# First norm's sums read apart from the keys', its factors turned by transposes, class-order factors from diagonals, first transfers reordered

## Chip, cores, metric

The kernel runs on one core of a Trainium2 chip. The metric is the device time of one execution in microseconds (us), the median of several.

## What is computed

Two transformer blocks follow one another on one sequence of 512 tokens with 1,024 features, all in float32. The part that the change touches is the first norm, the queries and keys of the first attention, and every later norm of the same form:

```python
h = rmsnorm(x, norm_mix_g[i])          # x * rsqrt(mean(x*x) + eps) * g
z = h @ w_in[i]                        # queries, keys, values, gates of both mixers
qa, ka, va, qb, kb, vb, ga, gb = jnp.split(z, split_at, axis=-1)
y_a = mixer_a(qa, ka, va, q_norm_g[i], k_norm_g[i], ...)   # q and k normed by head, rotary, 2 key heads
y_b = mixer_b(qb, kb, vb, rel_bias)    # dilated attention: token 4 l + r belongs to class r
x = x + (gate_a * y_a + gate_b * y_b) @ w_out[i]
# then a relu^2 MLP, an embedding gate, and the second block: SwiGLU, retention and
# differential attention, attention to a memory, SwiGLU, each behind an rmsnorm
```

## The kernel before

Features lie on the partitions, tokens along the free axis. A float32 product is made of three matmuls on halves of both operands: high by high (L637, or L646 where tokens are the output's partitions), high by low (L640, L649), low by high (L643, L652). ScalarE makes a weight's high half (L719), VectorE the low half (L728), a block of eight k-steps at a time (1 MB by SyncE's queue, two buffers each way). Block 0 holds the two key heads ("ka"), block 1 the values ("va", 32 steps of three 128x256 matmuls), block 2 the first two query heads.

The norm factor r of a token is not applied to x: projections are made of x times the gain, and r comes in when a product is drained. For the first norm ("mix") ScalarE squares the eight tiles of x (L1134), VectorE adds them into ACC (L1149, event x_acc). TensorE then turns ACC into sums, a column of 128 tokens at a time: four matmuls against a column of ones in token order (L932), four in class order, whose stationary operand is every fourth column of ACC (L936), and four for each key head (L942). All sixteen columns lie in PSUM bank 7 under one name, ("sums", "mix"), and VectorE reads them from L959 on, followed by a root by three Newton steps on 16 columns (L1018 to L1038). For the tile RB, which holds the factors of all 512 tokens on every partition, VectorE splits r in two halves and spreads the high half over the identity (`dve_rows`, L983 to L987), ScalarE does so with the low half (`act_rows`, L996), and TensorE multiplies both by a matrix of ones (L948, L951; for the keys L1275, L1278; L2099, L2102 for the two norms that share one place). ScalarE copies the result into RB (L1005). There are ten such pairs of row matmuls in the program: one each for mix, mlp, ple, mx2, mq and f2, one for each key head, and two for "both".

The order on every engine is written by hand. Each stream (a generator) yields a place, a number on the scale of the blocks, before its next instructions, and `weave` issues the instructions of the stream with the smallest place; `US` is a microsecond on that scale. So an instruction waits behind all that its engine has at smaller places. PSUM banks are claimed in the order of issue on TensorE:

```python
def claim(self, name, *banks):
    ...
    earlier = [self.before[b] for b in banks if b in self.before]
    for b in banks:
        self.before[b] = (self.sig.sem(f"free{own}"), self.turns[own])
    return earlier
```

The first writer of a new name waits until the last name in that bank has been drained (semaphore free7 for bank 7). `norm_place("mix")` is 1.88; the key heads' rotation starts at place 1.02 (`key_place`), with VectorE's steps L1211 and L1215 and ScalarE's L1185 (square), L1189 and L1190 (halves swapped), GpSimd's L1203.

SyncE issues the first transfers in `sp_begin`: the first quarter of the key weights, gains, second quarter, x tiles 1, 2 and 3, the other half of the weights, x tiles 4 to 7, block 1's weights, then small constants, the rotary table, the identity and ones, the bias selectors and table. ScalarE's queue brings x tile 0.

Of the kernel before, what the change touches and what calls it, by code (L numbers as in the profile page):

```python
# [10 lines left out]
R32 = mybir.dt.float32r  # L11
# [4 lines left out]
P = 128  # L16
# [237 lines left out]
class Kernel:  # L254
# [70 lines left out]
    def memory(self):  # L325
# [10 lines left out]
        self.RB, self.RBr, self.ACC = sb(86.5, [P, S]), sb(86.5, [P, S], R32), sb(88.5, [P, S])  # L336
        self.tmp = [sb(90.5 + 2 * i, [P, S])[:, :] for i in range(2)]
        self.tmp_r = [sb(90.5 + 2 * i, [P, S], R32)[:, :] for i in range(2)]
# [16 lines left out]
        self.qs_r = [pa(68 + 2 * i, [P, S], R32)[:, :] for i in range(2)]  # L355
        self.key_sq = [pa(76 + 2 * i, [P, S])[:, :] for i in range(2)]
        self.key_lo = [pa(80 + 2 * i, [P, S], R32)[:, :] for i in range(2)]
# [37 lines left out]
        self.ACC2, self.RB1, self.RB1r = pa(106, [P, S]), pa(108, [P, S]), pa(108, [P, S], R32)  # L395
# [39 lines left out]
        norm = lambda n: {"v": tiny(n), "r": tiny(n), "ev": tiny(n), "a": tiny(n), "h": tiny(n), "rh": tiny(4), "rl": tiny(4)}  # L435
        four = lambda: {k: tiny(4) for k in ("v", "r", "a", "h", "n")}
        self.nm = {"mix": norm(16), "mlp": norm(4), "ple": norm(4), "both": norm(8)}
        self.part, self.rh1, self.rl1 = tiny(4), tiny(4), tiny(4)
        self.ka_n = [{"rh": tiny(4), "rl": tiny(4)} for _ in range(2)]
# [483 lines left out]
    def pe_norm(self, pe, new, v, place, heads=()):  # L923

        yield place
        for w in new(self.at("ones"), *self.claim(("sums", v), 7)):
            pe.wait_ge(*w)
        out = self.bank(("sums", v))
        for w in new(self.absorbed(v, KT - 1)):
            pe.wait_ge(*w)  # L930
        for n in range(4):
            done = pe.matmul(out[:, n:n + 1], self.ACC[:, n * P:(n + 1) * P], self.ones[:, 0:1], start=True, stop=True)  # L932
        if heads:
            yield place + 0.12
            for n in range(4):
                pe.matmul(out[:, 4 + n:5 + n], class_of(self.ACC[:, :], n), self.ones[:, 0:1], start=True, stop=True)  # L936
            for j, sq in enumerate(heads):
                yield self.norm_place(v) + 0.06 * (j - 1)
                for w in new(self.at("head_sq", j)):
                    pe.wait_ge(*w)  # L940
                for i in range(4):
                    done = pe.matmul(out[:, 8 + 4 * j + i:9 + 4 * j + i], sq[:, i * P:(i + 1) * P], self.ones[:, 0:1], start=True, stop=True)  # L942
        done.then_inc(*self.full(("sums", v)))
        yield self.norm_place(v) + (6 if v == "mix" else 5) * US
        for w in new(self.at("rows_hi", v), *self.claim(("rows", v), 7)):
            pe.wait_ge(*w)
        out = self.bank(("rows", v))
        pe.matmul(out, self.ones_r, self.RBr[:, :], start=True, stop=False)  # L948
        for w in new(self.at("rows_lo", v)):
            pe.wait_ge(*w)  # L950
        pe.matmul(out, self.ones_r, self.tmp_r[0], start=False, stop=True).then_inc(*self.full(("rows", v)))  # L951

    def dve_norm(self, dve, new, v, place, rb_before):
# [4 lines left out]
        if v == "mix":  # L958
            dve.tensor_scalar(q["v"][:, 0:8], out[:, 0:8], 1.0 / D, EPS, ALU.mult, ALU.add).then_inc(*self.up("vector"))  # L959
            for w in new(self.sig.now("vector")):  # L960
                dve.wait_ge(*w)
            dve.tensor_scalar(q["ev"][:, 0:4], q["v"][:, 0:4], EPS, None, ALU.mult).then_inc(*self.up("ev", v))
            for w in new(self.at("ev", v)):
                dve.wait_ge(*w)
            for j in range(2):
                c = slice(8 + 4 * j, 12 + 4 * j)
                done = dve.scalar_tensor_tensor(out=q["v"][:, c], in0=out[:, c], scalar=1.0 / 128, in1=q["ev"][:, 0:4],
                                                op0=ALU.mult, op1=ALU.add)
            done.then_inc(*self.drained(("sums", v)))
        else:  # L970
            dve.tensor_scalar(q["v"], out[:, 0:4], 1.0 / D, EPS, ALU.mult, ALU.add).then_inc(*self.drained(("sums", v)))
        for w in new(self.cleared(("sums", v))):
            dve.wait_ge(*w)
        yield from self.dve_rsqrt(dve, new, q, place)
        for w in new(self.at("inverse", id(q))):
            dve.wait_ge(*w)
        yield from self.dve_rows(dve, new, q["rh"], q["rl"], q["r"][:, 0:4], self.RBr[:, :], ("rows_hi", v), ("rl_made", v),
                                 rb_before, place)

    def dve_rows(self, dve, new, rh, rl, r, rows, made, low_made, rows_before, place):  # L980

        yield place
        dve.tensor_scalar(rh.bitcast(R32), r, 1.0, None, ALU.mult).then_inc(*self.up("vector"))  # L983
        for w in new(self.sig.now("vector"), *rows_before):
            dve.wait_ge(*w)
        dve.tensor_tensor(rl, r, rh, ALU.subtract).then_inc(*self.up(*low_made))
        dve.tensor_tensor(by_token(rows), self.ident.unsqueeze(1).broadcast_to([P, 4, P]), spread4(rh),  # L987
                          ALU.mult).then_inc(*self.up(*made))

    def act_rows(self, act, new, rl, low_made, rows, made, rows_before, place):  # L990

        yield place
        for w in new(self.at(*low_made), *rows_before):
            act.wait_ge(*w)
        for i in range(4):
            done = act.activation(rows[:, i * P:(i + 1) * P], self.ident, ACT.Copy, scale=rl[:, i:i + 1])  # L996
        done.then_inc(*self.up(*made))

    def act_norm(self, act, new, v, place):
        yield from self.act_rows(act, new, self.nm[v]["rl"], ("rl_made", v), self.tmp_r[0], ("rows_lo", v),  # L1000
                                 [self.absorbed(v, 6)], place)
        yield place + (2.6 if v == "mix" else 2) * US
        for w in new(self.filled(("rows", v))):
            act.wait_ge(*w)
# [67 lines left out]
    def sp_begin(self, sp, new):  # L1072
# [36 lines left out]
    def act_begin(self, act, new):  # L1109
        yield -3.0  # L1110
        act.dma_start(self.X[:, 0:1, :], self.io["xT"].rearrange("(k p) s -> p k s", p=P)[:, 0:1, :]).then_inc(*self.up("x0", by=16))
        for w in new(self.at("zeros")):
            act.wait_ge(*w)
# [78 lines left out]
    def qs_free(self, n):  # L1192
# [3 lines left out]
        return self.filled(("rows_k", n - 2)) if n < 4 else self.at("joined", n - 2)  # L1196
# [2103 lines left out]
```

## Time and profile before

| | us |
|---|---|
| median of 3 runs | 2027.58 (2025.69 to 2027.70) |
| the profiled execution's own time | 2025.08 |
| its span in the profile | 2023.2 |
| TensorE busy | 2006.6, 99% of the span |
| VectorE busy | 1433.7, 71% |
| ScalarE busy | 989.0, 49% |
| GpSimd busy | 306.7, 15% |
| mean granted TensorE clock | 0.998 of full |

The profile is one execution. Busy time of TensorE counts a matmul until its last column has left the array, so consecutive matmuls overlap in it: the pace of the engine is the distance from start to start. Times of a row count from the start of the span.

### The profile page before, as it was taken

The numbers are of one execution on the slowest core, as the hardware profiler recorded it, in microseconds if no ns is written. First come the engines' busy times: TensorE is split into PE (matmuls) and PEld (weight loads), VectorE is DVE, ScalarE is ACT, GpSimd is POOL, SyncE is SP. The second block draws the span as 40 slices with busy tenths as digits, with TensorE's granted clock in tenths as the row PEclk, the third lists the DMA queues.
The fourth block names the chain that finished last, engine by engine and source line by source line (L and its number), as shares of the span: only waits on it lengthen the run. The fifth ranks groups of instructions, "written<-read, shape, count | busy, mean of one in ns | idle before, by whom it ended". The sixth has DMA issues, their size and how long they took to land.

```text
span 2023.2 us, 30620 instructions
## 1 busy us (share of the span) xinstructions
PE 2006.6 (99%) x11818; PEld 1758.6 (87%) x11818; DVE 1433.7 (71%) x2722; ACT 989.0 (49%) x1901; POOL 306.7 (15%) x494
## 2 busy tenths in 40 slices
PE   9999999999999999999999999999999999999998
PEld 8788898888889988888999989978898888999987
DVE  7886557676667776678788766676876668777765
ACT  6656334455445444555444434555554446444433
POOL 0230000021000000231011013422551021101110
PEclk9999999999999999999999999999999999999999
DMA  6141422122333333322323323222342123233341
GB/s 196 45 154 44 128 84 87 63 86 82 104 94 102 112 94 109 105 84 94 104 95 109 100 91 118 80 68 95 103 157 85 43 83 100 94 98 107 104 136 42
DMA packets 194665, 196.23 MB, mean 97 GB/s; under 512 B 5068, under 2 KB 189708, under 8 KB 194444
## 3 DMA queue, kind: packets, MB, share of 16 engines
q1 hardware_dynamic: 193800, 193.22, 29.8%
q8 instruction: 94, 1.54, 0.3%
q10 hardware_dynamic: 720, 1.05, 0.2%
q14 instruction: 51, 0.42, 0.1%
HBM read 192.05 MB, written 6.93 MB: 98 GB/s over the span
## 4 chain that ended last, share of the span: by engine, by line
PE 90%; DVE 5%; POOL 2%; issue 1%; ACT 1%; DMA 0%; SPq 0%; DVEq 0%; POOLq 0%; ACTq 0%
PE ps L700 19%; PE ps L637 18%; PE ps L643 18%; PE ps L640 18%; PE ps L646 3%; PE ps L649 3%; PE ps L652 3%; DVE m L728 1%; PE ps L1359 1%; PE ps L1657 1%; PE ps L1666 1%; PE ps L2260 0%; PE ps L1369 0%; PE ps L1371 0%; PE ps L1370 0%
## 5 line engine op out<-in xcount | busy, mean ns | idle before, releaser
L637 PE MATMUL ps<-m,m 128*128 128x512 f32 x1728 | 684.8, 396 | 0.0
L643 PE MATMUL ps<-m,m 128*128 128x512 f32 x1728 | 674.6, 390 | 0.2 <-DVE m L1161 0.2
L640 PE MATMUL ps<-m,m 128*128 128x512 f32 x1728 | 674.0, 390 | 0.0
L719 ACT ACTIVATE m<-m 128x512 fp32r<-128x512 f32 x512 | 306.8, 623 | 272.9 <-PE ps L643 234.4
L728 DVE TENSOR_TENSOR m<-m,m 128x512 fp32r<-128x512 f32 x512 | 382.2, 758 | 48.7 <-ACT m L719 47.0
L700 PEld LDWEIGHTS ps<-m,m 128*128 128x128 f32 x3276 | 398.3, 192 | 3.4 <-issue 0.4
L700 PE MATMUL ps<-m,m 128*128 128x256 f32 x3276 | 399.4, 283 | 0.2 <-ACT m L866 0.2
L643 PEld LDWEIGHTS ps<-m,m 128*128 128x128 f32 x1728 | 324.6, 188 | 70.8 <-DVE m L1161 1.1
L637 PEld LDWEIGHTS ps<-m,m 128*128 128x128 f32 x1728 | 325.4, 188 | 64.8 <-issue 1.5
L640 PEld LDWEIGHTS ps<-m,m 128*128 128x128 f32 x1728 | 325.5, 188 | 62.2 <-DVE m L728 0.3
L774 DVE TENSOR_TENSOR m<-m,m 128x512 fp32r<-128x512 f32 x273 | 198.8, 748 | 87.0 <-ACT m L764 86.5
L764 ACT ACTIVATE m<-m 128x512 fp32r<-128x512 f32 x273 | 159.6, 620 | 79.3 <-DVE m L787 25.8
L646 PE MATMUL ps<-m,m 128*128 128x256 f32 (+1 forms) x548 | 161.9, 295 | 0.0
L649 PE MATMUL ps<-m,m 128*128 128x256 f32 (+1 forms) x548 | 158.1, 289 | 0.5 <-DVE m L728 0.5
L652 PE MATMUL ps<-m,m 128*128 128x256 f32 (+1 forms) x548 | 157.9, 288 | 0.0
L1993 POOL TENSOR_TENSOR m<-m,m 128x512 f32<-128x512 f32 x44 | 75.3, 1713 | 531.8 <-DVE m L1960 284.8
L918 POOL TENSOR_TENSOR m<-m,m 128x512 f32<-128x512 f32 x35 | 47.9, 1369 | 459.6 <-ACT m L902 459.3
L646 PEld LDWEIGHTS ps<-m,m 128*128 128x128 f32 x548 | 104.7, 191 | 2.4 <-issue 0.4
L649 PEld LDWEIGHTS ps<-m,m 128*128 128x128 f32 x548 | 104.7, 191 | 2.5 <-DVE m L728 0.9
L652 PEld LDWEIGHTS ps<-m,m 128*128 128x128 f32 x548 | 104.5, 191 | 1.1
L866 ACT ACTIVATE m<-ps 128x256 f32<-128x256 f32 x117 | 44.8, 383 | 120.0 <-PE ps L700 120.0
L1785 DVE TENSOR_TENSOR m<-m,ps 128x512 f32<-128x512 f32 x72 | 49.2, 683 | 58.8 <-PE ps L643 58.7
(375 smaller groups left out, 2270.8 us busy)
## 6 DMA issues: line engine op xcount, KB each, us to landing
m<-ffn_w SPq DMA_DIRECT2D x44, 1024.0 KB, 5.1
m<-w_in SPq DMA_DIRECT2D x28, 1024.0 KB, 5.0
m<-ffn_w SPq DMA_DIRECT2D x24, 768.0 KB, 4.5
m<-w_ff SPq DMA_DIRECT2D x16, 1024.0 KB, 5.5
m<-w_ff SPq DMA_DIRECT2D x16, 768.0 KB, 4.4
m<-w_in SPq DMA_DIRECT2D x17, 512.0 KB, 5.0
m<-w_out SPq DMA_DIRECT2D x8, 1024.0 KB, 5.1
m<-mem_w_kv SPq DMA_DIRECT2D x8, 1024.0 KB, 5.4
```

The lines of the kernel that those rows point to most:

```text
L637: pe.matmul(o, lh, xh, start=k == 0, stop=False)
L640: pe.matmul(o, ll, xh, start=False, stop=False)
L643: done = pe.matmul(o, lh, xl, start=False, stop=k == nk - 1)
L646: pe.matmul(o, xh, wh[:, k, c:c + job.width], start=k == 0, stop=False)
L649: pe.matmul(o, xh, wl[:, k, c:c + job.width], start=False, stop=False)
L652: done = pe.matmul(o, xl, wh[:, k, c:c + job.width], start=False, stop=k == nk - 1)
L700: done = pe.matmul(out[half], weight[step == 1][c][:, k, :], xl if step == 2 else xh, start=a == 0 and c in (0, 1, 3), stop=a == 11 and c ...
L719: act.activation(self.WH[b % 2][:, at], self.RAW[b % 2][:, at], ACT.Copy).then_inc(*self.up("w_hi", b, c))
L728: dve.tensor_tensor(self.WL[b % 2][:, at], self.RAW[b % 2][:, at], self.WH[b % 2][:, at].bitcast(F32), ALU.subtract).then_inc(*self.up("w_ ...
L764: act.activation(self.split_slot(b, c, 0), src[c], ACT.Copy).then_inc(*self.up("w_hi", b, c))
L774: dve.tensor_tensor(self.split_slot(b, c, 1), src[c], self.split_slot(b, c, 0).bitcast(F32), ALU.subtract).then_inc(*self.up("w_lo", b, c))
L1993: pool.tensor_tensor(slot, slot, self.RB[:, :], ALU.mult).then_inc(*self.up("h_sum", name, t))
```

## The change

Five edits, in one diff:

- TensorE: the first norm's sums in token order are issued at place 1.42 instead of 1.65, under their own claim of bank 7; the four class-order sums are gone. The key heads' sums keep their places (1.82 and 1.88) but claim bank 7 under a new name, ("key_sums",).
- VectorE: the first norm's read-out and root are on 4 columns and stand at place 1.5, instead of after 1.95; the keys' (8 columns) stand after 1.95.
- The factors are spread by four transposes of one column broadcast to 128x128 (`turn_factors`), with no split in halves; `dve_rows` and `act_rows` are gone for all ten.
- The class-order factors are taken from RB's diagonals by four reductions on VectorE at place 3.6 (L1246).
- Transfers: x tile 1 goes by ScalarE's queue; SyncE waits for the first quarter of the weights before it issues the second half, and for x tiles 4 and 5 before it issues the small constants and what follows.

The diff, cut to what the text speaks of (other places change the names of tiles and columns alone):

```diff
-    def pe_norm(self, pe, new, v, place, heads=()):
+    def pe_norm(self, pe, new, v, place):
...
         for n in range(4):
             done = pe.matmul(out[:, n:n + 1], self.ACC[:, n * P:(n + 1) * P], self.ones[:, 0:1], start=True, stop=True)
-        if heads:
-            yield place + 0.12
-            for n in range(4):
-                pe.matmul(out[:, 4 + n:5 + n], class_of(self.ACC[:, :], n), self.ones[:, 0:1], start=True, stop=True)
-            for j, sq in enumerate(heads):
-                yield self.norm_place(v) + 0.06 * (j - 1)
...
         done.then_inc(*self.full(("sums", v)))
-        yield self.norm_place(v) + (6 if v == "mix" else 5) * US
-        for w in new(self.at("rows_hi", v), *self.claim(("rows", v), 7)):
+        yield self.norm_place(v) + (3 if v == "mix" else 5) * US
+        for w in new(self.at("inverse", id(self.nm[v])), self.at("consts"), *self.claim(("rows", v), 7)):
             pe.wait_ge(*w)
-        out = self.bank(("rows", v))
-        pe.matmul(out, self.ones_r, self.RBr[:, :], start=True, stop=False)
-        for w in new(self.at("rows_lo", v)):
-            pe.wait_ge(*w)
-        pe.matmul(out, self.ones_r, self.tmp_r[0], start=False, stop=True).then_inc(*self.full(("rows", v)))
+        self.turn_factors(pe, self.nm[v]["r"][:, 0:4], ("rows", v))
+
+    def turn_factors(self, pe, r, name):
+        for i in range(4):
+            done = pe.transpose(self.bank(name)[:, i * P:(i + 1) * P], r[:, i:i + 1].broadcast_to([P, P]), self.ident)
+        done.then_inc(*self.full(name))
...
+        dve.tensor_scalar(q["v"], out[:, 0:4], 1.0 / D, EPS, ALU.mult, ALU.add).then_inc(*self.drained(("sums", v)))
...
+    def act_norm(self, act, new, v, place, rb_before):
+        yield place + (-1 if v == "mix" else 2) * US
+        for w in new(self.filled(("rows", v)), *rb_before):
             act.wait_ge(*w)
         act.activation(self.RB[:, :], self.bank(("rows", v)), ACT.Copy).then_inc(*self.drained(("rows", v)))
...
-        sp.dma_start(self.X[:, 1:2, :], x[:, 1:2, :]).then_inc(*up("x1", by=16))
         sp.dma_start(self.X[:, 2:4, :], x[:, 2:4, :]).then_inc(*up("x2", by=16))
+        for w in new(self.at("first_w0")):
+            sp.wait_ge(*w)
         sp.dma_start(raw[:, 4:8, :], w0[:, 4:8, :]).then_inc(*up("first_w2", by=16))
...
         yield -0.9
+        for w in new(self.at("x4")):
+            sp.wait_ge(*w)
         sp.dma_start(self.G[:, n:], io["smalls"][:, n:]).then_inc(*up("smalls", by=16))
...
+        act.dma_start(self.X[:, 1:2, :], ...).then_inc(*self.up("x1", by=16))     # in act_begin, behind x tile 0
...
+    def pe_key_sums(self, pe, new):
+        for j, sq in enumerate(self.key_sq):
+            yield self.norm_place("mix") + 0.06 * (j - 1)
+            if j == 0:
+                for w in new(*self.claim(("key_sums",), 7)):
+                    pe.wait_ge(*w)
...
+    def dve_key_norm(self, dve, new, place):
+        yield place
+        q, out = self.key_n, self.bank(("key_sums",))
+        for w in new(self.filled(("key_sums",)), self.at("ev", "mix")):
+            dve.wait_ge(*w)
...
+        yield from self.dve_rsqrt(dve, new, q, place)
+
+    def dve_class_factors(self, dve, new, place):
+        yield place
+        for w in new(self.rb_made("mix"), self.filled(("sums", "mix"))):
+            dve.wait_ge(*w)
+        for c in range(4):
+            done = dve.tensor_tensor_reduce(self.ACC[:, c * P:(c + 1) * P], class_of(self.RB[:, :], c), self.ident, 1.0, 0.0, ALU.mult,
+                                            ALU.add, self.class_r[:, c:c + 1])
...
-        s += [self.pe_norm(pe, new, v, 1.65 if v == "mix" else self.norm_place(v), heads=self.key_sq if v == "mix" else ()) for v in self.NORMS]
+        s += [self.pe_norm(pe, new, v, 1.42 if v == "mix" else self.norm_place(v)) for v in self.NORMS]
+        s += [self.pe_key_sums(pe, new)]
...
-        s += [self.dve_norm(dve, new, v, self.norm_place(v) + 0.8 * US, self.rb_before(v)) for v in self.NORMS]
+        s += [self.dve_norm(dve, new, v, 1.5 if v == "mix" else self.norm_place(v) + 0.8 * US) for v in self.NORMS]
+        s += [self.dve_key_norm(dve, new, self.norm_place("mix") + 0.8 * US), self.dve_class_factors(dve, new, 3.6)]
```

How the order moves on TensorE between the class-order sums and the first key head's sums. Line numbers of the changed kernel are three lower here; m_91 and m_86 are the first key head's squares, full, free and the like the semaphores waited for. Before:

```order
L652 MATMUL ps<-m_54,m_50 128x256
L936 MATMUL ps<-m_58,m_63 128x1 x4
L646 MATMUL ps<-m_54,m_49 128x256
L649 MATMUL ps<-m_56,m_49 128x256
L652 MATMUL ps<-m_54,m_50 128x256
L646 MATMUL ps<-m_54,m_49 128x256
L649 MATMUL ps<-m_56,m_49 128x256
L652 MATMUL ps<-m_54,m_50 128x256
L942 MATMUL ps<-m_58,m_91 128x1 [waits head_sq]
L942 MATMUL ps<-m_58,m_91 128x1 x3
```

Changed (39 matmuls of the value projection lie between the token-order sums and these rows):

```order
L649 MATMUL ps<-m_54,m_50 128x256
L643 MATMUL ps<-m_54,m_49 128x256
L646 MATMUL ps<-m_56,m_49 128x256
L649 MATMUL ps<-m_54,m_50 128x256
L1221 MATMUL ps<-m_58,m_86 128x1 [waits head_sq,free7]
L1221 MATMUL ps<-m_58,m_86 128x1 x3
```

The class-order sums are gone, and the key sums wait for one semaphore more, free7, in the same place among the projection's matmuls.

VectorE around the read-out of the first norm's sums (L959 before, L947 now). m_60 is the tile of small columns, m_55 the low half of block 2's weights. Before:

```order
L1211 TENSOR_TENSOR m_86<-ps,m_84 128x512 [waits swap,full1]
L1215 TENSOR_TENSOR m_85<-m_85,m_87 128x512 [waits free0,turned]
L1174 TENSOR_SCALAR m_83<-m_83,m_59 128x512 x2
L728 TENSOR_TENSOR m_55<-m_51,m_53 128x512 [waits w_hi]
L1215 TENSOR_TENSOR m_86<-m_86,m_88 128x512 [waits free1,turned]
L728 TENSOR_TENSOR m_55<-m_51,m_53 128x512 [waits w_hi] x2
L959 TENSOR_SCALAR m_60<-ps 128x8 [waits full7]
```

Changed:

```order
L1167 TENSOR_TENSOR m_83<-ps,m_81 128x512 [waits swap,full1]
L1171 TENSOR_TENSOR m_82<-m_82,m_84 128x512 [waits free0,turned]
L1130 TENSOR_SCALAR m_80<-m_80,m_59 128x512 x2
L725 TENSOR_TENSOR m_55<-m_51,m_53 128x512 [waits w_hi]
L1171 TENSOR_TENSOR m_83<-m_83,m_85 128x512 [waits free1,turned]
L947 TENSOR_SCALAR m_60<-ps 128x4 [waits full7]
L951 TENSOR_SCALAR m_60<-m_60 128x4 [waits free7]
```

The read-out stands two weight subtractions earlier, directly behind the second key head's rotation; all that is ahead of that is unchanged.

## Rows read from the trace of the kernel before

**Rows 1.** The page: busy time of each engine and its share of the span.

```profile
PE 2006.6 (99%) x11818; PEld 1758.6 (87%) x11818; DVE 1433.7 (71%) x2722; ACT 989.0 (49%) x1901; POOL 306.7 (15%) x494
```

**Rows 2.** Waits of TensorE, first 70 us (total, times, longest).

```profile
PE ps L1223 <- DVE m L1254: 0.4, 1, 0.4
PE ps L1359 <- DVE m L1397: 0.4, 1, 0.4
```

**Rows 3.** Chain that ended last (start us, us, what), first 50 us.

```profile
28.56 1.75 PE ps L936 x8
...
31.13 0.79 PE ps L942 x8
...
36.90 0.68 DVE m L987
...
46.04 0.14 issue
46.18 1.02 PE ps L1223 x8
```

**Rows 4.** Timeline of TensorE, 23 to 46 us (start us, us, engine, line, ...).

```profile
23.55 0.28 PE L646 MATMUL ps<-m,m 128*128 128x256 f32 x1
...
30.96 0.28 PE L942 MATMUL ps<-m,m 128*128 128x1 f32 x2
...
45.35 0.39 PE L643 MATMUL ps<-m,m 128*128 128x512 f32 x1
```

**Rows 5.** Timeline of VectorE, 20 to 34 us.

```profile
21.35 1.48 DVE L1149 TENSOR_TENSOR m<-m,m 128x512 f32<-128x512 f32 x2
26.08 0.69 DVE L1211 TENSOR_TENSOR m<-ps,m 128x512 f32<-128x512 f32 x1 [3.25 <-ACT m L1190]
...
31.07 0.68 DVE L1215 TENSOR_TENSOR m<-m,m 128x512 f32<-128x512 f32 x1
31.67 1.28 DVE L728 TENSOR_TENSOR m<-m,m 128x512 fp32r<-128x512 f32 x2
33.55 0.17 DVE L959 TENSOR_SCALAR m<-ps 128x8 f32<-128x8 f32 x1 [0.60 <-PE ps L942]
```

**Rows 6.** Timeline of ScalarE, 21 to 28 us.

```profile
24.12 0.63 ACT L719 ACTIVATE m<-m 128x512 fp32r<-128x512 f32 x1 [2.74 <-DMA m<-w_in]
```

**Rows 7.** Timeline of SyncE and ScalarE at the start: issues, and work on x tile 4.

```profile
10.71 1.34 ACT L1119 ACTIVATE m<-m,m 128x512 fp32r<-128x512 f32 x2 [0.74 <-DMA m<-xT]
...
13.52 0.37 SPq L879 DMA_DIRECT2D m<-w_in  x1
```

**Rows 8.** Timeline of TensorE: row matmuls, and four transposes in the attention.

```profile
39.32 0.39 PE L948 MATMUL ps<-m,m 128*128 128x512 f32 x1
...
39.77 0.39 PE L637 MATMUL ps<-m,m 128*128 128x512 f32 x1
...
61.31 0.60 PE L1359 MATMUL ps<-m,m 128*128 128x128 f32 x4
61.67 0.48 PE L637 MATMUL ps<-m,m 128*128 128x512 f32 x1
```

**Rows 9.** Weight loads of L1359 (busy us, mean ns).

```profile
L1359 PEld LDWEIGHTS ps<-m,m 128*128 128x128 f32 x128 | 15.7, 140 | 5.2 <-issue 1.4
```

**Rows 10.** VectorE in the attention (59 to 65 us), and its nearest reduction by form.

```profile
59.55 0.51 DVE L1392 TENSOR_SCALAR m<-m,m 128x512 f32<-128x512 f32 x1
...
64.90 0.69 DVE L1215 TENSOR_TENSOR m<-m,m 128x512 f32<-128x512 f32 x1 [1.69 <-POOL m L1203]
...
L2308 DVE DVE_READ_ACCUMULATOR2_ANT m<- 128x1 f32 x32 | 2.6, 82 | 0.0
...
L2308 DVE CUSTOM_DVE_ANT_0 m<-ps,m 128x128 f32<-128x128 f32 x8 | 2.3, 286 | 0.9 <-PE ps L2260 0.9
```

**Rows 11.** TensorE at the norm for two users; windows (PE busy ... clock).

```profile
888.25 2.09 PE L2093 MATMUL ps<-m,m 128*128 128x1 f32 x16 [0.89 <-issue]
...
890.20:893.30 3.10, 3.10 (x8) 2.46 (x9) 2.40 (x16) 0.00 (x0) 0.00 (x0) 0.51 0.91 312
```

More of the change, by code:

```diff
@@ L972, in dve_norm @@
         for w in new(self.cleared(("sums", v))):
             dve.wait_ge(*w)
+        if v == "mix":
+            dve.tensor_scalar(q["ev"], q["v"], EPS, None, ALU.mult).then_inc(*self.up("ev", v))
         yield from self.dve_rsqrt(dve, new, q, place)
[L975 to L988, printed above, removed]
@@ L1259, in dve_key_a @@
             *self.up("head_lo", j))
+    def pe_key_sums(self, pe, new):
[4 more added lines that the diff above has]
+                    pe.wait_ge(*w)
+            for w in new(self.at("head_sq", j)):
+                pe.wait_ge(*w)
+            for i in range(4):
+                done = pe.matmul(self.bank(("key_sums",))[:, 4 * j + i:4 * j + i + 1], sq[:, i * P:(i + 1) * P], self.ones[:, 0:1], start=True,
+                                 stop=True)
+        done.then_inc(*self.full(("key_sums",)))
+    def dve_key_norm(self, dve, new, place):
[3 more added lines that the diff above has]
+            dve.wait_ge(*w)
+        for j in range(2):
+            c = slice(4 * j, 4 * j + 4)
+            done = dve.scalar_tensor_tensor(out=q["v"][:, c], in0=out[:, c], scalar=1.0 / 128, in1=self.nm["mix"]["ev"], op0=ALU.mult,
+                                            op1=ALU.add)
+        done.then_inc(*self.drained(("key_sums",)))
+        for w in new(self.cleared(("key_sums",))):
+            dve.wait_ge(*w)
[3 more added lines that the diff above has]
+        for w in new(self.rb_made("mix"), self.filled(("sums", "mix"))):
+            dve.wait_ge(*w)
+        for c in range(4):
+            done = dve.tensor_tensor_reduce(self.ACC[:, c * P:(c + 1) * P], class_of(self.RB[:, :], c), self.ident, 1.0, 0.0, ALU.mult,
+                                            ALU.add, self.class_r[:, c:c + 1])
+        done.then_inc(*self.up("vector", "class_r"))
     def act_key_a(self, act, new, j, place):
         yield from self.act_rotate(act, new, ("ka", j), j, self.key_sq[j], [], place)
-        yield from self.act_rows(act, new, self.ka_n[j]["rl"], ("rl_k", j), self.key_lo[j], ("rows_k_lo", j), [],
-                                 self.norm_place("mix") + (4.6 + j) * US)
         yield self.norm_place("mix") + (9 + 1.5 * j) * US
@@ L1271, in pe_key_a @@
         yield self.norm_place("mix") + (7 + 1.5 * j) * US
-        for w in new(self.at("rows_k_hi", j), *self.claim(("rows_k", j), 6 + j)):
+        for w in new(self.at("inverse", id(self.key_n)), self.at("consts"), *self.claim(("rows_k", j), 6 + j)):
             pe.wait_ge(*w)
-        out = self.bank(("rows_k", j))
-        pe.matmul(out, self.ones_r, self.qs_r[j], start=True, stop=False)
-        for w in new(self.at("rows_k_lo", j)):
-            pe.wait_ge(*w)
-        pe.matmul(out, self.ones_r, self.key_lo[j], start=False, stop=True).then_inc(*self.full(("rows_k", j)))
+        self.turn_factors(pe, self.key_n["r"][:, 4 * j:4 * j + 4], ("rows_k", j))
     def act_values(self, act, new, name, r, r_made, before, place, parts):
@@ L2094, in pe_norm_both @@
         done.then_inc(*self.full(("sums", "both")))
-        for name, rows, low, at in ((("rows", "both"), self.RBr, self.tmp_r[0], 4), (("rows", "last"), self.RB1r, self.tmp_r[1], 6)):
+        q = self.nm["both"]
+        for name, r, at in ((("rows", "both"), q["r"][:, 0:4], 4), (("rows", "last"), q["r"][:, 4:8], 6)):
             yield place + at * US
-            for w in new(self.at("rows_hi", name[1]), *self.claim(name, 7)):
+            for w in new(self.at("inverse", id(q)), *self.claim(name, 7)):
                 pe.wait_ge(*w)
-            pe.matmul(self.bank(name), self.ones_r, rows[:, :], start=True, stop=False)
-            for w in new(self.at("rows_lo", name[1])):
-                pe.wait_ge(*w)
-            pe.matmul(self.bank(name), self.ones_r, low, start=False, stop=True).then_inc(*self.full(name))
+            self.turn_factors(pe, r, name)
     def dve_norm_both(self, dve, new, place):
```

90 lines of the change are left out of this document (21 added, 69 removed).

## The prediction

> **What bounds the kernel.** I read the page first: TensorE is busy 2006.6 of 2023.2 us [rows 1], so what counts is its own work and the places where it stands. Of 2025.08 us for the profiled execution, 2023.2 lie in the span; the median of the three runs is 2.5 above it, and the runs lie 2.0 apart. A measurement of this kernel can tell 0.2%, or 4.1 us, from no change. The waits of TensorE over the first 70 us come next: the only two of them behind the norm are 0.4 us each [rows 2]. Then the chain, to see whose work is on the path (28.56 to 33.5 us: TensorE's sums) [rows 3], and the timelines of TensorE, VectorE and ScalarE over 20 to 34 us, to see who would be early or late once rows move [rows 4 to 6]. Elsewhere the norms' steps on VectorE and ScalarE lie beside a TensorE that doesn't wait for them: no row matmul has a wait, so the nine other splits that go (a 128x512 product on VectorE, four small copies on ScalarE each) are costed at nothing; what covers them is the projection behind each norm, and fewer of them leaves the cover whole.
>
> **Class-order sums.** Four sums in class order go: 1.75 us of the chain [rows 3]. TensorE then reaches the first key head's sums not at 30.96 [rows 4] but at 30.96 - 1.75 = 29.2. That is the gain, if nothing waits. (The token-order sums only change places with projection matmuls: place 1.42 is reached at 23.55 [rows 4], and ACC is complete at 21.35 + 1.48 = 22.83 [rows 5], so they don't wait.)
>
> **The wait added.** The key sums now claim bank 7 under a name of their own, so they wait for the token-order sums to be read out of it. That read-out stands on VectorE directly behind the second key head's L1215, and nothing ahead of it moves. VectorE stands idle from 22.8 to 26.08 for ScalarE's swapped halves [rows 5]; ScalarE itself is held by block 2's weights, which land at 24.1 [rows 6]; from 26.08 VectorE works without a gap up to L1215 at 31.07, and takes its next instruction at 31.67 [rows 5]. So the read-out runs at 31.67 to 31.84 (0.17, as L959 [rows 5]), and TensorE starts 0.14 later, as behind L1254 [rows 3]: at 31.98. It is ready at 29.2, so it stands 2.8 us, and the key sums come 31.98 - 30.96 = 1.02 us later than before. The gain is inside this wait. Behind the waiting instruction on TensorE's queue lie the rest of the value projection and block 2, that is, everything.
>
> **Given back.** Before, the first query head's sums waited for L1254 (they start at 46.18 [rows 3]). The matmul ahead of them started at 45.35 [rows 4] and at the pace below would have let them go at 45.58, so 0.6 us were lost there. Now the keys' root follows on VectorE at 35.5 and takes some 2.6 us, without splitting and spreading (three products of 0.6 us); the keys' rows are due on TensorE at 42, the bank is free about 45.3, and TensorE comes at 45.58 + 1.02 = 46.6. No wait: net **+0.4 us**.
>
> **Transposes for row matmuls.** Two row matmuls take 39.32 to 39.77, 0.45 us, 0.227 each. Four transposes take 61.31 to 61.67, and the matmul behind them is busy 0.48 instead of 0.39: 0.45 in all [rows 8]. For ten sets the difference is nothing. But no row has a stationary operand with step 0, one column broadcast over 128. Its bounds: the contiguous load of L1359, 140 ns [rows 9], and the load of every fourth column: the class-order sums took 1.75 against 0.79 for contiguous ones [rows 3], 0.96 over eight loads or 0.12 each, so 40 loads would add 4.8 us. I take L1359's, which is the same instruction on the same identity; the upper end goes into the range. The Trainium skill ("SBUF — State Buffer", Door 1, on cachelines) says that accesses within one 16-byte line run at full rate and that each new line costs; by it step 4 is slow and step 0 is not, and the sum would be the one with nothing added. No run here shows step 0 yet.
>
> **Class factors on VectorE.** Four reductions of 128x128 with the read of their sum: the nearest rows take 0.29 and 0.08 [rows 10], so 1.5 us together, up to 2.3 if the read with step 4 is as slow on VectorE as on TensorE's loads. They stand just ahead of the softmax of the first query head, where the row at 59.55 [rows 10] releases transposes at 61.31 [rows 8]. With +0.4 and 1.5 they release at 59.55 + 0.51 + 1.9 + 0.14 = 62.1, TensorE is ready at 61.7: 0.4 us of wait, and about as much at the fourth score matmul, whose bank the delayed exponential frees. VectorE's 1.69 us of idleness at 64.90, for GpSimd [rows 10], then takes the delay up, and TensorE's wait of 0.4 for L1397 [rows 2] shrinks as TensorE comes later. Of some 0.8 I keep **+0.2**; ends 0 and +1.0.
>
> **First transfers.** All that they can do to TensorE before 29.2 is hidden by its 2.8 us wait, a gain as well as a loss below 2.8. What isn't hidden is when block 2's weights land, for ScalarE waits for them [rows 6]. SyncE issues them at 13.52 [rows 7]. With the new wait for x tile 4, which had landed by 10.71 [rows 7], five issues of about 0.5 us follow: 13.2, still in time. The bytes ahead are the same, and with a megabyte of block 1 still due the queues have work meanwhile. I cost this at nothing, between -0.5 and +0.5.
>
> **The clock.** At 889.9 the granted clock fell from 2.4 to 1.2 GHz, after TensorE had stood 0.9 us and had then run 2.0 us of one-column sums; in the 3.1 us that followed it made 8 matmuls where 13 fit [rows 11], a loss of 1.3 to 1.5 us. The change makes a like stretch at 29.2: 2.8 us of standing, then 0.8 of sums. So I expect one more fall at 32 to 34 us, less what lies under the sums: **+1.3**; ends 0 and +1.6. Sum: 0.4 + 0.2 + 1.3 = +1.9. The profiled span becomes 2025.1, its time 2027.0, and the median 2027.58 + 1.9 = **2029.5**.
>
> **Rivals.**
> - No fall of the clock: +0.6, 2028.2. For it: the first norm's own sums (0.8, 1.75, 0.8, 0.8 us with matmuls between) passed at full clock. Against it: nothing there stood.
> - The gain arrives: VectorE comes to the read-out by 29.2 because block 2's weights land over 2 us sooner, or the wait isn't there. -1.75 + 0.2: 2026.0. Against it: the bytes ahead are the same.
> - Slower: broadcast columns load at the pace of step 4. From 0.06 us a load on, 40 loads with +1.9 leave the band of 4.1. At 0.12, +6.7: 2034.3. Against it: VectorE's product L987, which reads columns with step 0, takes 0.68 [rows 3], and L1215 without them 0.68 too [rows 5].
> - Slower: transposes let the clock fall at each of the seven later norm stages but one where it fell already. 6 x 1.4 = 8.4 and 1.9: 2037.9. Against it: the 128 transposes of L1359 [rows 9] run in a stretch without a fall; of the whole span's clock, 0.998 of full, the one fall at 889.9 is all. A set lasts 0.4 us, with matmuls on both sides. The Trainium skill ("TensorE: Matmul & The Clock Gate", Part 4) says that a transpose doesn't count as busy for the clock; by it this rival would have more weight.
> - It doesn't do what it says: the class factors keep VectorE so long that the transposes wait more than 1 us; +3, 2030.6.
>
> **Chances.** Forecast 0.50, no fall 0.22, gain 0.10, slow loads 0.08, clock at each norm 0.03, class factors 0.07. The range that holds 0.8 takes in the first three and the last, with the 2.0 us between equal runs: 2026.0 to 2032.0. Faster by over 4.1 (below 2023.5) needs the gain and the fall at 890 gone too: 0.04. Slower by over 4.1 (above 2031.6): slow loads, the clock, and an edge of the forecast: 0.13. Within: 0.83.
>
> **What would show it.** In the changed profile: TensorE waits 2.8 us at L1221 for VectorE L947; L947 at 31.7; no wait at the query sums L1179 (46.6); the clock at 0.50 for some 3 us from 32 to 34; weight loads of L939 at 140 ns; L1246 near 0.29; block 2's first L716 at 24.1. I am wrong if L1221 starts near 29.2, if L939's loads are over 200 ns, or if the total moves by over 4 us.

## The result, and the profile after

| | before | changed |
|---|---|---|
| median of 20 executions each, us | 2025.69 (2024.86 to 2029.56) | 2031.78 (2026.85 to 2034.23) |
| ratio to before, 95% interval | | 1.0024 (1.0019 to 1.0030) |
| the same once more, on another occasion, 11 executions | 2027.34 | 2029.62; 1.0014 (1.0005 to 1.0023) |
| profiled span, us; mean granted clock | 2023.2; 0.998 | 2030.5; 0.995 |

The change is slower: by 4.9 us (3.8 to 6.1) in the first comparison and 2.8 us (1.0 to 4.7) in the second. These differences and their intervals come from the ratio, which is formed over all executions; the bare medians lie 6.1 and 2.3 us apart. The forecast was +1.9. Up to the key sums TensorE has nearly the same work in both kernels, so the loss can be followed by where a line of the one stands in the other.

Waits of TensorE over the first 80 us of the changed kernel (total, times, longest), to be held against [rows 2]:

```profile
PE ps L1221 <- DVE m L947: 3.9, 1, 3.9
PE ps L1061 <- POOL m L1054: 1.0, 1, 1.0
PE ps L1342 <- DVE m L1380: 0.6, 1, 0.6
PE ps L634 <- DVE m L1111: 0.6, 1, 0.6
PE ps L646 <- DVE m L725: 0.5, 2, 0.2
PE ps L634 <- ACT m L1075: 0.4, 1, 0.4
```

The forecast wait is first, 3.9 us instead of 2.8, and the wait at the first query sums ([rows 2], L1223) is gone, as forecast. L1342's wait grew from 0.4 to 0.6. L1061's is the same 1.0 us in both kernels (L1106 before), L646's too (L649 before). L634's two (the first x tiles) are new; they lie ahead of the long one and mostly shorten it: TensorE is ready for the key sums at 30.3, not at the 29.2 of the prediction.

The timeline of TensorE (start, us, line) shows the stand and what the matmuls behind it take:

```profile
30.04 0.28 PE L649 MATMUL ps<-m,m 128*128 128x256 f32 x1
34.23 1.05 PE L1221 MATMUL ps<-m,m 128*128 128x1 f32 x8 [3.90 <-DVE m L947]
...
35.68 0.41 PE L649 MATMUL ps<-m,m 128*128 128x256 f32 x1
...
36.53 1.70 PE L1221 MATMUL ps<-m,m 128*128 128x1 f32 x8
...
51.97 0.95 PE L1179 MATMUL ps<-m,m 128*128 128x1 f32 x8
```

The key sums start 3.3 us later than in [rows 4]. From then on a matmul that took 0.28 takes 0.41, and eight matmuls of the sums take 1.70, for 0.95 in the kernel before. The windows say why (span of the window; PE, PEld, DVE, ACT, POOL busy; granted clock):

```profile
35.20:42.02 6.82, 6.82 (x29) 6.43 (x29) 5.16 (x24) 0.63 (x1) 0.00 (x0) 0.50 0.48 151
895.36:902.19 6.83, 6.83 (x20) 5.57 (x20) 4.73 (x19) 0.00 (x0) 0.00 (x0) 0.50 0.48 154
```

The clock was at 1.2 GHz from 35.20 to 42.02 us, where before it was at 2.4, and at 895.36 it stayed there for 6.83 us, where before it did so from 889.85 for 3.41 [rows 11]. The ledger of the profiled span: +3.3 at the key sums, 0.6 given back at the query sums, some 3 lost at half clock (half of 6.8, less what hides in loads and small sums), which gives the first query sums at 51.97 instead of 46.18, +5.8; and 1.5 more at the second fall: +7.3, the difference of the spans. The last 1.5 belong to this one execution: a second profile of the changed kernel (after_again, below) has no fall at this place at all, and those of old_transfers and filler have one of 3.41 us there, like the kernel before.

Why the stand is 3.9 us long is on the chain of the changed kernel (start, us, what; DVEq is VectorE's queue, issue a step that waits for nothing the profile shows):

```profile
14.57 11.89 DMA m<-w_in
26.47 0.02 issue
26.49 0.63 ACT m L716
27.12 0.02 issue
27.15 0.59 ACT m L1145
27.74 0.02 issue
27.76 0.60 ACT m L1146
28.36 0.04 DVEq L1166
28.40 0.04 issue
28.44 0.69 DVE m L1167
29.14 1.13 DVE m L725
...
34.10 0.08 DVE m L947
34.19 0.04 issue
34.23 1.05 PE ps L1221 x8
```

Block 2's weights land at 26.47. ScalarE's high half of them (L716) stands ahead of the key's swapped halves (L1145, L1146); VectorE's rotation follows (L1167 and what is behind it), then the read-out (L947), then the key sums. [Rows 6] had ScalarE's start at 24.12; the 2.4 us between them arrive unchanged at L947 (34.02 for the 31.67 forecast). A transfer sits on the critical path that in the kernel before was not near it.

### The profile page after: what moved, and what is told of

Same layout as the page of the kernel before. It is cut to its first block, busy times and chain, and to the rows that moved or that the text cites. A ratio compares the mean times of both kernels' runs of the same rounds, so it can differ in the third digit from the quotient of the medians.

```text
span 2030.5 us, 30583 instructions
## 1 busy us (share of the span) xinstructions
PE 2009.3 (99%) x11830; PEld 1760.6 (87%) x11830; DVE 1428.5 (70%) x2712; ACT 977.4 (48%) x1861; POOL 307.8 (15%) x494
## 4 chain that ended last, share of the span: by engine, by line
PE 90%; DVE 5%; POOL 2%; issue 1%; DMA 1%; ACT 1%; DVEq 0%; SPq 0%; POOLq 0%; ACTq 0%
PE ps L697 19%; PE ps L634 18%; PE ps L640 18%; PE ps L637 18%; PE ps L643 3%; PE ps L649 3%; PE ps L646 3%; DMA m<-w_in 1%; DVE m L725 1%; PE ps L1342 1%; PE ps L1640 1%; PE ps L1649 1%; PE ps L2231 0%; PE ps L1352 0%; PE ps L1354 0%
## 5 line engine op out<-in xcount | busy, mean ns | idle before, releaser
L634 PE MATMUL ps<-m,m 128*128 128x512 f32 x1728 | 686.5, 397 | 1.0 <-DVE m L1111 0.6
L716 ACT ACTIVATE m<-m 128x512 fp32r<-128x512 f32 x512 | 306.7, 624 | 278.7 <-PE ps L640 235.3
L634 PEld LDWEIGHTS ps<-m,m 128*128 128x128 f32 x1728 | 325.9, 189 | 66.0 <-issue 2.3
L761 ACT ACTIVATE m<-m 128x512 fp32r<-128x512 f32 x273 | 159.6, 620 | 79.5 <-DVE m L784 25.7
L646 PE MATMUL ps<-m,m 128*128 128x256 f32 (+1 forms) x548 | 158.8, 290 | 0.5 <-DVE m L725 0.5
L649 PE MATMUL ps<-m,m 128*128 128x256 f32 (+1 forms) x548 | 158.6, 289 | 0.0
L646 PEld LDWEIGHTS ps<-m,m 128*128 128x128 f32 x548 | 105.4, 192 | 2.4 <-DVE m L725 0.9
L649 PEld LDWEIGHTS ps<-m,m 128*128 128x128 f32 x548 | 105.3, 192 | 1.1
```

What stands on the lines that cost most here:

```text
L634: pe.matmul(o, lh, xh, start=k == 0, stop=False)
L646: pe.matmul(o, xh, wl[:, k, c:c + job.width], start=False, stop=False)
L649: done = pe.matmul(o, xl, wh[:, k, c:c + job.width], start=False, stop=k == nk - 1)
L716: act.activation(self.WH[b % 2][:, at], self.RAW[b % 2][:, at], ACT.Copy).then_inc(*self.up("w_hi", b, c))
L761: act.activation(self.split_slot(b, c, 0), src[c], ACT.Copy).then_inc(*self.up("w_hi", b, c))
```

## Experiments

**Take the wait away: early_read.** The read-out goes ahead of the first key head's rotation, into the stretch where VectorE is idle for ScalarE; the root stays.

```diff
         if v == "mix":
             dve.tensor_scalar(q["ev"], q["v"], EPS, None, ALU.mult).then_inc(*self.up("ev", v))
-        yield from self.dve_rsqrt(dve, new, q, place)
+            yield 1.5
+        yield from self.dve_rsqrt(dve, new, q, 1.5 if v == "mix" else place)
...
-        s += [self.dve_norm(dve, new, v, 1.5 if v == "mix" else self.norm_place(v) + 0.8 * US) for v in self.NORMS]
+        s += [self.dve_norm(dve, new, v, 1.02 if v == "mix" else self.norm_place(v) + 0.8 * US) for v in self.NORMS]
```

> Changed kernel with one move: VectorE reads the token-order sums (L947) and makes the small product (L951) ahead of the first key head's rotation instead of behind the second's; the root stays where it was, at place 1.5. Theory (the wait for bank 7 and the clock's fall behind it make the loss): TensorE reaches the key sums at 34.23 - 3.90 = 30.3 us and does not wait there; no stretch at half clock behind it (it lasted 6.8 us from 35.2, so some 3 us come back), the stand of 3.9 us goes, of which 0.6 to 0.7 is lost again at the first query sums. So 0.5 to 1.5 us under the kernel before: 2024 to 2025.5 where before shows 2025.7. Rival A (the clock falls because of something else of the change, the transposes or the transfers): the half clock stays, and the time is 1.5 to 3 us above before. Rival B (another wait takes its place, head_sq or the second half of block 2's weights, 2.4 us late): the key sums start at 32 or later and the time stays within 1 us of the changed kernel's.

Measured: 2024.14 us, 0.9985 of before (0.9976 to 0.9994). Its timelines, VectorE's read-out and TensorE's key sums and first transposes:

```profile
25.43 0.16 DVE L947 TENSOR_SCALAR m<-ps 128x4 f32<-128x4 f32 x1 [1.70 <-PE ps L929]
```

```profile
30.01 0.95 PE L1222 MATMUL ps<-m,m 128*128 128x1 f32 x8
31.62 0.95 PE L1222 MATMUL ps<-m,m 128*128 128x1 f32 x8
37.07 0.62 PE L939 MATMUL ps<-m,m 128*128 128x128 f32 x4 [1.26 <-DVE m L1234]
```

The stand is gone, the key sums take 0.95, and there is no half clock before the end of the program. The theory holds, rivals A and B fall. Two instructions of 0.16 us, which stood behind the second key head's rotation, eight instructions later on VectorE, are worth 5.5 us against after_again (2029.62; another occasion). The gain over the kernel before, 3.0 us (1.2 to 4.9), is larger than the 0.5 to 1.5 expected. Part of it may be the clock near 890, where this profile has no fall and the kernel before has one of 3.41 us; no run separates that. A new wait of 1.3 us came in at L939, for L1234, which empties bank 7.

**The transfers: old_transfers, old_transfers_early_read, before_new_transfers.** The first two undo the transfer edit (x tile 1 back on SyncE's queue, both waits out), without and with the early read; the third makes that edit alone in the kernel before.

```diff
+        sp.dma_start(self.X[:, 1:2, :], x[:, 1:2, :]).then_inc(*up("x1", by=16))
         sp.dma_start(self.X[:, 2:4, :], x[:, 2:4, :]).then_inc(*up("x2", by=16))
-        for w in new(self.at("first_w0")):
-            sp.wait_ge(*w)
...
-        for w in new(self.at("x4")):
-            sp.wait_ge(*w)
```

> Changed kernel with the transfers of the kernel before: x tile 1 on SyncE's queue, and SyncE waits for nothing. Theory (the two waits of SyncE delay block 2's weights from 24.1 to 26.5 us, and through ScalarE's swapped halves, VectorE's rotation and the read-out the wait at bank 7): the weights land at 24.1, the read-out stands at 31.7, TensorE waits 2.8 us instead of 3.9, key sums at 32.0. The time comes 2 to 3 us down, to 1.5 to 3.5 above before. Rival (transfers are hidden as the prediction said, weights late for another reason): weights at 26, wait 3.9, no change against the changed kernel.

> Both edits together: transfers of before, and the read-out ahead of the first key head's rotation. Theory: no stand at the key sums, which start at 30.96 - 1.75 = 29.2; of the 1.75 us some 0.6 to 1 is given back at the first query sums (bank read-out by L1215's line), class factors cost 0 to 0.5. 0.5 to 1.5 us under before, and below early_read by the 0.3 to 1.1 us that the first x tiles and weights come sooner. Rival (the class factors and transposes cost what was gained): within 0.3 us of before or above it.

> Kernel before with the new transfers alone (x tile 1 on ScalarE's queue, SyncE waits for the first weights and for x tile 4). Theory: block 2's weights land at 26.4, but TensorE's key sums wait only for the squares, so the delay of 2.4 us is mostly slack there; it costs the 0.3 to 1.1 us of TensorE's late start, less what the first query sums' wait gives back: 0 to +1.0 us against before, no new stretch at half clock. Rival (late transfers cost by themselves): +2 to +4 us, with a wait of TensorE for block 2's halves or the keys' rotation.

Measured, against before in the same comparison: old_transfers 2030.71 us, 1.0016 (1.0008 to 1.0025); old_transfers_early_read 2022.88, 0.9979 (0.9970 to 0.9988), under both kernels; before_new_transfers 2026.26, 0.9998 (0.9989 to 1.0006). The first two differ in the place of the read-out alone and were measured side by side: 7.8 us. Timeline of TensorE and windows of old_transfers:

```profile
29.43 0.28 PE L649 MATMUL ps<-m,m 128*128 128x256 f32 x1
33.25 1.87 PE L1217 MATMUL ps<-m,m 128*128 128x1 f32 x8 [3.54 <-DVE m L947]
...
36.40 1.70 PE L1217 MATMUL ps<-m,m 128*128 128x1 f32 x8
```

```profile
29.70:33.25 3.55, 0.01 (x2) 0.01 (x1) 3.52 (x8) 1.08 (x3) 0.88 (x1) 0.83 0.01 2
33.25:42.26 9.01, 9.01 (x37) 8.53 (x38) 6.00 (x30) 0.63 (x1) 0.00 (x0) 0.50 0.36 116
```

And of ScalarE:

```profile
25.49 0.63 ACT L716 ACTIVATE m<-m 128x512 fp32r<-128x512 f32 x1 [3.67 <-DMA m<-w_in]
```

The stand is 3.54 us, not the 2.8 expected, though nothing of the transfers differs from before. Its block 2 weights let ScalarE start at 25.49, not at 24.12 [rows 6], and that is the 1.4 us by which its read-out (33.05) misses 31.67. The same row in the other profiles shows how far one execution can be trusted. Those with the old order have 24.12 (before), 25.49, 25.21, 25.28, 25.70, 25.27, 24.71; those with the new have 26.49, 25.81, 26.99, 26.59, 26.82, 26.36. Means 25.11 and 26.51: the edit costs 1.4 us at this landing, and the other 1.0 us of the 2.4 was the luck of the one execution I had read. In the kernel before the edit costs nothing measurable in the median, though in the profile of before_new_transfers TensorE stands 0.9 us at L1279 for ScalarE, where the kernel before has no wait. In the profile of old_transfers the clock fell during the stand itself, at 32.02 and so ahead of the sums, for 10.24 us. The expected 2 to 3 us under the changed kernel aren't shown: 1.0016 of before lies between that kernel's two ratios, 1.0024 and 1.0014.

**after_again.** The changed kernel itself, unedited.

> The changed kernel once more, beside the other three and on their chip, so that landings, the granted clock and medians can be compared within one set. If block 2's weights land at 26.4 again, the late landing belongs to the change; if they land between 25 and 26, up to 1 us of it is scatter between executions. Time: 4 to 6 us over before. Rival: 2 us or less over before, the first comparison having caught slow executions.

Measured: 2029.62 us, 1.0014; landing 26.59, stand 3.24, half clock from 34.84 for 6.83 us. The late landing repeats; the loss, 2.8 us, lies between the two expectations (4 to 6, and 2 or less).

**The clock apart from the stand: filler, filler_22.**

```diff
             if j == 0:
+                for _ in range(16):
+                    pe.matmul(self.ps[:, 6, :], self.ones_r, self.xg["mix"].hi[0], start=True, stop=True)
                 for w in new(*self.claim(("key_sums",), 7)):
```

> Changed kernel with 16 matmuls of 128x512 (3.6 us at 0.227) into the unused bank 6, issued right ahead of the wait for bank 7, their results read by nobody. The stand is replaced by work; the key sums start as late as before. Theory (the clock falls because TensorE stands): the granted clock stays at full through 35 to 42 us, the key sums' 8 columns keep 0.95 us, and the time is 3 us under the changed kernel though the key sums start no earlier: 1.5 to 2.5 us over before. Rival A (the one-column sums let the clock fall): the half clock stays, and the time too. Rival B (the stand alone is the loss, the clock makes little): same time as the changed kernel.

> As filler, with 22 matmuls (5.0 us) ahead of the wait for bank 7, since in filler TensorE still stood 1.1 us behind the 16 and the profiled execution still fell to half clock at 36.35 us, though only 3 of its 11 executions had a mean clock of 0.997 and the others 0.998 or more. Theory (standing lets the clock fall): no stand at L1223 and no half clock near 35 us in the profile; the key sums start at 34.4 to 35.2. Time within 1 us of filler's. Rival (the one-column sums alone suffice): half clock from 35 or 36 us again.

Measured: filler 2026.98 us, 2.6 under after_again beside it, 1.0001 of before (0.9992 to 1.0010), though its key sums start at 34.60. filler_22, on another occasion: 2027.75, 1.0007 (0.9998 to 1.0016). The key sums of filler, then the useless matmuls and the key sums of filler_22:

```profile
34.60 1.05 PE L1223 MATMUL ps<-m,m 128*128 128x1 f32 x8 [1.15 <-DVE m L947]
```

```profile
30.14 5.18 PE L1217 MATMUL ps<-m,m 128*128 128x512 f32 x22
35.16 0.95 PE L1223 MATMUL ps<-m,m 128*128 128x1 f32 x8
```

The window of filler_22 over the place of the fall:

```profile
31.00:46.00 15.00, 15.00 (x86) 13.02 (x86) 11.20 (x41) 5.30 (x12) 0.46 (x1) 1.00 0.23 72
```

Full clock throughout, with the same one-column sums in it and no stand: in this execution the sums alone don't bring the fall. Giving TensorE useless work until the bank is free thus saves 2.6 of the 5.5 us that lie between the changed kernel and early_read; the rest, by subtraction, goes with the late key sums themselves. By filler_22 the saving is smaller, 1.4 us between the ratios 1.0014 and 1.0007, but its key sums start 0.56 us later than filler's and the two intervals overlap. The two estimates of the clock's price are thus 1.4 and 2.6 us of the median, the latter measured side by side. Filler's profiled execution still stood 1.15 us and fell at 36.35; its other executions mostly didn't (8 of 11 have a mean clock of 0.998 or more, of the changed kernel's 31 none).

**The sums at 890: sums_apart**, made from best (below).

```diff
         for i in range(8):
+            if i in (2, 4, 6):
+                yield place + 0.12 * i
```

> The kernel best, with the 8 columns (16 matmuls, 1.9 us) of the sums at the norm for two users (L2073, L2076 here) issued in four pairs with projection matmuls between. There the clock fell at 889.8 in best and in before, behind 0.7 to 0.9 us of standing and 1.9 to 2.1 of one-column sums. Theory (dense small matmuls behind a stand count as little work): no fall at 890 in the profile, more executions at a mean clock of 0.999, median 0.3 to 1.0 us under best's 0.9981 of before. Rival (the stand alone, or the place in the program, makes it fall): fall at 890 as before, same time.

Measured: 2028.36 us, 1.0008 (0.9999 to 1.0017), some 5 us over best (0.9981, on another occasion). The spacing was chosen too wide. Timeline of TensorE:

```profile
886.09 0.58 PE L2075 MATMUL ps<-m,m 128*128 128x1 f32 x4 [0.68 <-issue]
...
895.83 0.50 PE L2075 MATMUL ps<-m,m 128*128 128x1 f32 x4
899.23 0.65 PE L939 MATMUL ps<-m,m 128*128 128x128 f32 x4 [2.90 <-DVE m L991]
```

The last sums come 8 us later, the root with them, and the transposes stood 2.9 us. The clock didn't fall at 890, with the same stand of 0.7 us ahead, but at 900.56, behind the new stand. That says nothing of the dense sums at 890. Four other profiled kernels (early_read, old_transfers_early_read, after_again, filler_22) kept them dense, 1.9 us behind a stand of 0.7, and have no fall there either; nine have one. What makes it fall there in one execution and not in another stays open.

**Transposes: best, double_turns.** best is old_transfers_early_read with the first norm's transposes due later (first diff); double_turns is best with each set made twice (second diff).

```diff
-        yield self.norm_place(v) + (3 if v == "mix" else 5) * US
+        yield self.norm_place(v) + 5 * US
...
-        yield place + (-1 if v == "mix" else 2) * US
+        yield place + (1.4 if v == "mix" else 2) * US
```

```diff
-        for i in range(4):
+        for i in (0, 1, 2, 3, 0, 1, 2, 3):
```

> Transfers of before, read-out ahead of the first key head's rotation, and the first norm's transposes due 5 us instead of 3 us behind the norm's place (ScalarE's copy into RB with them), because in old_transfers_early_read TensorE waited 1.0 us at L939 for VectorE L1230, which empties bank 7. Theory: that wait goes and the time falls by 0.5 to 1.0 us below old_transfers_early_read, 4.5 to 5.5 us under before (2021.5 to 2022.5). Rival: the first query sums then wait as before the change (0.4 us) and the gain is under 0.3 us.

> The kernel best, with every set of four transposes of a broadcast column made twice, the second over the first: 40 transposes more. Theory (a transpose of a step-0 column costs what L1342's does, a set 0.44 us on the path): +4.4 us against best, no new stretch at half clock. If the sets were hidden beside other work: under +2. Rival (the broadcast column loads slowly, or transposes let the clock fall): +6 or more, with half clock behind the norms.

Measured: best 2023.12 us, 0.9981 (0.9972 to 0.9990), against 0.9979 of old_transfers_early_read on another occasion: L939's wait is gone, and the median doesn't show it. That is the rival's outcome, by another way, for no wait came at the query sums. Its profiled execution had a fall at 889.83 that old_transfers_early_read's had not. double_turns: 2027.37, +4.25 for 40 transposes, 0.106 each, against 4.4 expected. The loads with step 0 (PEld, mean ns):

```profile
L939 PEld LDWEIGHTS ps<-m,m 128*128 128x128 f32 x80 | 9.2, 136 | 1.2
```

They are as fast as [rows 9]. The one stretch at half clock ahead of the program's end is that from 890.75 for 3.41 us, as in the kernel before.

**Class factors: class_later.**

```diff
-        ... self.dve_class_factors(dve, new, 3.6)]
+        ... self.dve_class_factors(dve, new, b["vb0"] - 1)]
```

> The kernel best, with the four class-order reductions on VectorE (1.3 us) moved from place 3.6, ahead of the first query head's softmax, to one block ahead of the second mixer's values. Theory (they delay the probabilities and cost 0.2 us): TensorE's wait at L1339 falls from 0.64 back to 0.4 us, the span is 0.2 us shorter, not measurable in the median. Rival (they cost 0.5 to 1 us, in several waits of the score matmuls): L1176's later places move 0.5 us or more ahead against best's from 49.59.

Measured: 2022.88 us, 0.9982 (0.9973 to 0.9991). The wait at L1339 is 0.43 instead of 0.64. Head sums that stood 0.81 us apart from best's ahead of the place (48.78 and 49.59) stand 1.06 apart behind it (68.13 and 69.19): the reductions cost 0.25 us.

**Which wait of SyncE: best_late_issue.** To best, the wait for x tile 4 alone.

```diff
+        for w in new(self.at("x4")):
+            sp.wait_ge(*w)
         sp.dma_start(self.G[:, n:], io["smalls"][:, n:]).then_inc(*up("smalls", by=16))
```

> The kernel best, with one of the changed kernel's transfer edits put back: SyncE waits for x tiles 4 and 5 before it issues the small constants and block 2's weights. Theory (this wait is what makes block 2's weights late: 26.5 to 27.0 in the kernels with the new transfers, 24.1 to 25.7 in those with the old): ScalarE's first L716 on them starts at 26.3 or later, and since nothing waits for the read-out there the time stays within 0.5 us of best. Rival (the other edits, x tile 1 on ScalarE's queue and the wait for the first weights, delay everything by pushing the second half of the weights back): L716 at 25.2 to 25.7 as in best.

Measured: 2023.09 us, 0.9978 (0.9969 to 0.9986). Timeline of ScalarE:

```profile
24.73 0.63 ACT L716 ACTIVATE m<-m 128x512 fp32r<-128x512 f32 x1 [2.96 <-DMA m<-w_in]
```

ScalarE starts on block 2 at 24.73, within the range of the old order. My theory falls, as far as one profile can tell: this wait alone doesn't delay the weights, though the constants are issued only from 11.08 on. What is left is the wait for the first weights or x tile 1 on the other queue; in the changed kernel they put the issue of the second half of the first weights (L1037) at 4.86, for 3.39 before. Timeline of SyncE in the changed kernel:

```profile
4.86 0.37 SPq L1037 DMA_DIRECT2D m<-w_in  x1
...
6.34 0.47 SPq L876 DMA_DIRECT2D m<-w_in  x1
11.77 0.34 SPq L1043 DMA_DIRECT2D m<-smalls  x1
...
14.57 0.38 SPq L876 DMA_DIRECT2D m<-w_in  x1
```

The last of these is block 2, a microsecond later than in [rows 7]. ScalarE starts on it 11.9 us after that, for 10.85 in best, which issues it at 14.43. A later issue is thus not the whole delay: over the seven kernels with the old order and the six with the new the issue is at 13.95 and 14.60 in the mean, 0.65 of the 1.4 us, and filler, issuing at 14.04, has its weights only at 26.8. Which of the two remaining edits does it, or whether the three work together, stays open.

## Why the prediction was right, and where not

The range, 2026.0 to 2032.0, held both medians, and that was in part luck. It was built on 2027.58, the median of three runs of the kernel before; 20 executions give 2025.69. As a difference it ran from -1.6 to +4.4 us around +1.9. The second comparison, +2.8 (1.0 to 4.7), lies in it; the first, +4.9 (3.8 to 6.1), doesn't, and by the prediction's own last sign (a total that moves by over 4 us) the forecast was wrong there. The likeliest class (within 0.2%) holds the second comparison and misses the first by a little. The direction and the mechanism, a wait for the read-out of bank 7 and a fall of the clock behind it, were right; both were sized too small.

- **Class-order sums** (-1.75): right. From the last wait for block 1's low halves to the key sums it is 10.26 us in before_new_transfers and 8.42 in early_read, which differ there by these sums: 1.84.
- **The wait added**: the mechanism, its partner L947 and its place were right, with 2.8 us mis-sized: 3.9, 3.2 and 3.5 in three profiles. The key sums came at 34.23, not at 31.98; the stand grew by only 1.1 us of these 2.25, since TensorE reached it 1.1 us later than worked out. The step that failed is the one that took block 2's landing, 24.1, from one execution as fixed. The other six profiled kernels with the same transfers have it 0.6 to 1.6 later, and the transfer edit adds 1.4.
- **Given back** (-0.6): right, no wait at the query sums.
- **Transposes** (0, up to +4.8): right at 0. A set costs 0.42, the row matmuls took 0.45. The rule of the Trainium skill ("SBUF — State Buffer", Door 1) on cachelines agrees: 136 ns with step 0, for 140 contiguous.
- **Class factors** (+0.2): right, 0.25; the reductions took 0.37 and 0.07 each, 1.3 us together for the 1.5 worked out.
- **First transfers** (0, to +0.5): wrong, +1.4 at block 2's landing. "The bytes ahead are the same" and "13.2, still in time" were the failed steps. The wait for the first quarter put off the x tiles too: SyncE's wait for tiles 4 and 5 ended near 11.8 instead of 10.7, the five issues behind it took 2.8 us and not 2.5, block 2 was issued at 14.57, and it took longer to land. And I had used the stand as a cover for the transfers, while their last one fed the stand.
- **The clock** (+1.3): the fall came, at 35 rather than 32 to 34, and twice as long. I had taken the price from one row of 3.4 us; falls of 3.4, 6.8 and 10.2 us occur. By filler against after_again it is 2.6 us of the median. The likeness to the stretch at 890 was weak ground: with the same stand and sums the clock fell there in some profiles and not in others. The ground that held is the stand: all three profiles with a stand of 3.2 to 3.9 us ahead of the key sums have a fall, one from within it. A stand of 1.15 us with the sums behind it (filler) had one too, and one of 1.26 us ahead of transposes (early_read) none, so how short a stand suffices stays open. The rule of the Trainium skill ("TensorE: Matmul & The Clock Gate", Part 4) that transposes don't count as busy shows no effect in these runs: best is at full clock over its first twelve transposes (37.7 to 42.6 us), and the 40 further ones of double_turns brought no further fall.
- **"The gain arrives"** (0.10) was judged rightly for this change, by the wrong reason: not the bytes but the place of one read-out decided it. With it moved and the old transfers the kernel runs 4.2 us under before.

## To carry to other kernels

When two groups of results that shared a PSUM bank get names of their own, look where the first one's read-out stands in the reading engine's order, and put it into an idle stretch ahead of the second group's turn. A stand of TensorE of 3.2 to 3.9 us cost close to double here, by the clock behind it. And a landing read from one execution is a sample: take its spread from other executions before you let a cover of 1 or 2 us rest on it.

## What the runs showed that was not expected

- The scatter between equal executions of one kernel goes with TensorE's clock. The 98 executions of the kernel before in the three later comparisons: 52 with a mean clock of 0.998 have a median of 2025.65 us, 32 with 0.997 have 2027.74, 14 with 0.995 have 2029.41. A fall of one profile may be missing in the next execution: the one at the norm for two users, near 890 to 895 us, is there in nine of the thirteen profiles that keep its sums dense. So a sum of 1 or 2 us can't be checked on one trace.
- The clock can fall in the first microseconds too: in after_again at 7.53 us, for 3.41, behind a stand of 1.1 us for an x tile.
- With one and the same order of issue, ScalarE could start on block 2's weights at anything from 24.1 to 25.7 us, in one execution each of seven kernels.
